# Low parts of 24 weight units moved from GpSimd to VectorE, between GpSimd's indirect DMAs, and TensorE's key units written as loops

## The chip, the core and the metric

The kernel runs on one core of a Trainium2 chip. The metric is the device time of one execution in microseconds (us). Engines are named as in the profile: PE is TensorE, DVE VectorE, ACT ScalarE, POOL GpSimd, SP SyncE (it only issues DMAs here). "L509" is line 509 of the kernel before.

## The reference, cut to what matters

Two transformer blocks over 512 tokens of width 1024, in float32. The change lies in the second half of the first block, a product-key expert layer:

```
q = (ht @ wq).reshape(T, 8, 2, 128)                 # T = 512 tokens
sc = einsum('thpd,hpnd->thpn', q, subkeys)          # 128 scores for each half key
v1, i1 = top_k(sc[:, :, 0], 16);  v2, i2 = top_k(sc[:, :, 1], 16)
best, pos = top_k(v1[..., :, None] + v2[..., None, :], 16)     # 16 experts of each head
experts = e1 * 128 + e2                             # of 16384
gates = softmax(best)
u = u_tab[experts];  vv = v_tab[experts]
act = gelu(einsum('tkd,td->tk', u, x));  out = einsum('tk,tkd->td', gates * act, vv)
```

The kernel does not gather rows of `u_tab`. It computes `gelu(x . u)` of all 16384 experts for all tokens (the **key pass**), and then adds up all rows of `v_tab` weighted by gate times activation (the **value pass**), where the gates stand in a dense, mostly zero table in DRAM. Only for the first 128 tokens does it fetch rows instead. So the gates of the other 384 tokens have to be scattered into that table before the value pass.

## The kernel before, in words

**Units.** Every weight matrix is cut into units of 128 x 1024 float32 (512 KB). Unit `u` goes through a ring of eight buffers: SP loads `raw` (L440) once PE has used unit `u-8`, ACT makes the high part `hi` (L1062, `split_hi`), and POOL or DVE makes the low part `lo = raw - hi`. PE multiplies in three passes, high by high, high by low and low by high (`mm3`, L593 to L595). One unit of the key pass (`project`) is 24 matmuls with 512 columns. ACT writes the gelu of its result to `stage` (L1264, `gelu(u)`), and then makes the high part of unit `u+5`. PE may start unit `u` when the low part of `u` is there and the gelu of `u-4` is done.

**The key pass** is 128 units, `U_PEER` to `U_PEER + 127`; below they are key units 0 to 127. Low parts of key units 0 to 27 (`LOW_FROM` = 28) are POOL's, in four quarters of 256 columns (L509). From 28 on they are DVE's (L1765, `unit_low`), in one instruction, except for the 24 units of the list `BESIDE` (30, 34, 38, 42, 47, 51, ... 123, 127), which are POOL's.

**DVE** has an order written out by hand. It selects the experts of each group of 128 tokens, in the order 1, 2, 3, 0: `select(t, between)` finds the 16 best, and `join_gates(t, between)` sums the gates of equal experts and makes the scatter's addresses; its last step is `gates_made` (after L1863). `between` says how many key units' low parts are made at each step (`lows(n)`). ACT does an exp in between for each `t`, after the gelus of units 5, 17, 29 and 45. After the last select, DVE takes one low part and two parts of the second block's modulation (`ada_part`, L1781 and L1783, on weights that SP loads beside the units) for each unit from 56 on. PE sums these up in between (`ada_sum`, L786), twelve times.

**POOL** issues 384 indirect DMAs (`scatter`, L547), one for each `t` in 1 to 3 and each of 128 slots, each with 128 values of 4 bytes. They come in 24 groups of 16 (`SCATTERS`): a group waits for `gates_made` of its `t`, or for the landing of the group before it of the same `t`. The first five groups are of t = 1, 2, 1, 2, 3. Behind every fourth DMA of a group stands a quarter of the low part of that group's `BESIDE` unit; at the first quarter POOL waits for the high part of that unit.

**The end of the key pass.** After the gelu of unit 124 (`LOADS_AT`) ACT waits for all 384 scatters, then issues the first loads of gates and activations (L1274, L1280), and only then does the gelus of units 125 to 127. DVE multiplies gates by activations (L1921) and makes their low part (L1927), after which PE can start the value pass. PE's value pass is a loop of eight units (`pe.Fori(0, P // RING - 2)`, 14 rounds) between eight units written out at each end. The key pass is written out in full. Then POOL picks activations (L533) and fetches rows (L541) for the first 128 tokens, and the second block follows.

Of the kernel before, what the change touches and what calls it, by code (L numbers as in the profile page):

```python
# [16 lines left out]
F32 = mybir.dt.float32  # L17
# [4 lines left out]
ALU = mybir.AluOpType  # L22
AX_X = mybir.AxisListType.X

P = 128
D = 1024
DC = D // P
# [30 lines left out]
U_DIFF = U_PEER + 2 * P  # L58
# [19 lines left out]
EXP_AT = (5, 17, 29, 45)  # L78
SCATTERS = [(1, 0), (2, 0), (1, 1), (2, 1)] + [s for h in range(6) for s in ((3, h), (1, h + 2), (2, h + 2))] \
    + [(3, 6), (3, 7)]  # L80
BESIDE = [30 + 17 * n // 4 for n in range(len(SCATTERS))]
ZEROS = 8
LOADS_AT = P - 4
BUNCH = 4
# [34 lines left out]
def build_program(nc, w_units, x_in, ctx_in, params, consts, consts2, trig, pool_w, subkeys, ada_w, out,  # L119
                  rel_dram, gate_dram, act_dram, x_dram):  # L120
    KB = 1024
    with ExitStack() as ctx:
# [381 lines left out]

        @block.gpsimd
        def _(pool):
            def quarter(u, part):
                cols = slice(part * (D // 4), (part + 1) * (D // 4))
                return nc.gpsimd.tensor_tensor(lo[:, u % RING, cols], raw[:, u % RING, cols],  # L509
                                               hi[:, u % RING, cols].bitcast(F32), ALU.subtract)  # L510

            def low_part(u, per=0, i=None):

                pool.wait_ge(hi_ready, u + 1 if i is None else i * per + (u + 1))
                for part in range(4):
                    last = quarter(u, part)
                last.then_inc(lo_ready, 1)

            def low_range(a, b):
# [31 lines left out]
            nc.gpsimd.memset(zero[:, :], 0.0).then_inc(zero_made, 1)  # L551
            low_range(0, U_PEER + LOW_FROM)
            pool.wait_ge(zeroed, 16 * ZEROS)
            for n, (t, h) in enumerate(SCATTERS):
                if h == 0:
                    pool.wait_ge(gates_made, t)
                else:
                    pool.wait_ge(scattered[t - 1], 16 * TOPK * h)
                for k in range(TOPK):
                    scatter(t, TOPK * h + k)  # L560
                    if k % 4 == 3:
                        if k == 3:
                            pool.wait_ge(hi_ready, U_PEER + BESIDE[n] + 1)
                        last = quarter(U_PEER + BESIDE[n], k // 4)
                last.then_inc(lo_ready, 1)
            pool.wait_ge(mine_at, 2)
            pool.wait_ge(unit_used, U_VALUES)
            for s in a_stored:
# [15 lines left out]
        def _(pe):  # L584
# [11 lines left out]

            def unit_in(u, per=0, i=None):
                made, n = lo_ready, u + 1
                before = sum(U_PEER + b < u for b in BESIDE)
                if u - U_PEER in BESIDE:  # L600
                    n = U_PEER + LOW_FROM + before + 1
                elif U_PEER + LOW_FROM <= u < U_DIFF + LAG:
                    made, n = value_lo_ready, u + 1 - (U_PEER + LOW_FROM) - before
                elif u >= U_DIFF + LAG:
                    n -= U_DIFF + LAG - (U_PEER + LOW_FROM) - before
                pe.wait_ge(made, n if i is None else i * per + n)

            def project(u, dst, ah, al, per=0, i=None, ready=None):

                unit_in(u, per, i)  # L610
                for c in range(DC):
                    if ready is not None:
                        pe.wait_ge(ready[0], ready[1] + c + 1)
                    wh, wl = unit_chunk(u, c)
                    last = mm3(dst, wh, wl, ah[:, c], al[:, c], c == 0, c == DC - 1)
                last.then_inc(unit_used, 1)
# [157 lines left out]
            scores(2 * PEER_HEADS - 1)  # L774


            def ada_sum(s):

                pe.wait_ge(ada_used, DC * (s + 1))
                if s >= 2:  # L780
                    pe.wait_ge(ada_turned, s - 1)
                sides = range(2 if s < 2 else 1)
                for v in sides:
                    rows = acc[:, s % 2, v].rearrange("p (b q r) -> p q b r", q=4, r=32)
                    for q in range(4):
                        last = mm(ps[32 * q:32 * q + 32, 6 + s % 2, 0:2 * P].rearrange("p (b r) -> p b r", r=32),  # L786
                                  pick_c[:, v, :], rows[:, q], start=v == 0, stop=v == sides[-1])
                last.then_inc(ada_summed, 1)

            pe.wait_ge(cact_ready, 1)  # L790
            for u in range(P):
                if u >= 4:
                    pe.wait_ge(gel_done, u - 3)
                project(U_PEER + u, ps[:, u % 4, :], hn_hi, hn_lo)
                if u == CTX_SQUARE + DC + 2:
                    pe.wait_ge(sq_added, (DC - 1) * (WHOLE[3] + 1))
                    mm(ps[:, 4, 0:TC], ones, csq[:, 0, :], start=True, stop=True).then_inc(mean_ready, 1)
                s, after = (u - ADA_LOW - 3) // 4, (u - ADA_LOW - 3) % 4
                if s == 0 and after == 0:
                    pe.wait_ge(tk_done, 2 * PEER_HEADS)  # L800
                if after == 0 and 0 <= s < SECTIONS:
                    ada_sum(s)

            def value_unit(v, i=None, first=False, final=False):

# [708 lines left out]
        def _(dve):  # L1514
# [285 lines left out]
            def lows(n):  # L1800

                for u in range(key_lows[0], min(key_lows[0] + n, P + LAG)):
                    if u not in BESIDE:
                        unit_low(U_PEER + u)
                key_lows[0] += n

            def select(t, between):
# [80 lines left out]
            select(1, 0)  # L1888
            join_gates(1, (0,) * 7)
            select(2, 0)  # L1890
            join_gates(2, (0, 0, 0, 0, 0, 0, 1))
            select(3, 2)
            join_gates(3, (1, 1, 2, 1, 1, 2, 1))
            select(0, 2)
# [450 lines left out]
```

## Time and profile before

| | |
|---|---|
| median of 3 runs | 3061.32 us (3044.7 to 3061.61) |
| the profiled execution | 3072.2 us, its span 3070.4 us |
| PE busy | 2875.8 us (94%) |
| DVE busy | 1762.4 us (57%) |
| POOL busy | 1704.7 us (56%) |
| ACT busy | 983.9 us (32%) |
| mean granted clock of PE | 0.968 |

The span is from the first to the last instruction; times in views count from its start. A row of the view by lines names line, engine, operation, tiles written and read, their count, then busy time and mean duration, then the idle time before them and what ended it. Spans of POOL are rough, but the start of one indirect DMA to the start of the next is not.

### The profile page before, as it was taken

How to read it: one execution, taken by the hardware profiler on the slowest of the kernel's cores; microseconds unless marked ns; L12 is line 12 of the kernel's file. 1: busy time of each engine (PE TensorE's matmuls, PEld its weight loads, DVE VectorE, ACT ScalarE, POOL GpSimd, SP SyncE). 2: the span in 40 equal slices, each digit the busy share in tenths (PEclk: the TensorE clock that was granted, in tenths of full speed). 3: DMA queues.
4: the chain of work that ended last, by engine and by line, in shares of the span. 5: the costliest groups of instructions: out<-in, count | busy, mean ns of one | idle time of the engine just before them, and what ended most of it. 6: DMA issues, size and time to landing. Idle time of an engine off the chain costs nothing.

```text
span 3070.4 us, 39204 instructions
## 1 busy us (share of the span) xinstructions
PE 2875.8 (94%) x14484; PEld 2443.1 (80%) x14484; DVE 1762.4 (57%) x2726; ACT 983.9 (32%) x1472; POOL 1704.7 (56%) x1757
## 2 busy tenths in 40 slices
PE   8799988888989988999999989999999989999999
PEld 6698877677777778999999858558888868898887
DVE  6568997665553136778887773674333353343333
ACT  4432322222222333333333433783322222232211
POOL 5144877788888755688753123002554545555553
PEclk9899999999999999999999999999999999999999
DMA  6932443378875467999997211101323323233332
GB/s 202 342 97 83 153 129 98 122 250 284 289 267 186 124 209 283 325 338 347 355 350 276 90 55 50 38 1 59 97 90 102 96 76 96 72 108 103 97 95 75
DMA packets 191662, 499.40 MB, mean 163 GB/s; under 512 B 29608, under 2 KB 80936, under 8 KB 190888
## 3 DMA queue, kind: packets, MB, share of 16 engines
q1 hardware_dynamic: 104528, 338.95, 33.4%
q10 hardware_dynamic: 52184, 91.23, 8.4%
q0 software_dynamic: 34816, 67.41, 6.3%
q8 instruction: 86, 1.41, 0.2%
q14 instruction: 48, 0.39, 0.0%
HBM read 432.82 MB, written 64.68 MB: 162 GB/s over the span
## 4 chain that ended last, share of the span: by engine, by line
PE 57%; POOL 21%; DVE 11%; issue 6%; ACT 3%; DMA 2%; another core or an unknown queue 0%; SPq 0%; ACTq 0%; DVEq 0%
PE ps L593 17%; PE ps L595 17%; PE ps L594 17%; POOL gate_dram L547 13%; POOL value_rows L541 3%; POOL picked L533 3%; POOL unit_lo L509 3%; PE ps L917 2%; DVE nb L2000 1%; PE ps L937 1%; DMA unit_raw<-w_units 1%; DVE same L1858 1%; DVE same L1856 1%; DVE gate_sums L1860 1%; PE ps L928 1%
## 5 line engine op out<-in xcount | busy, mean ns | idle before, releaser
L509 POOL TENSOR_TENSOR unit_lo<-unit_raw,unit_hi 128x256 fp32r<-128x256 f32 x1112 | 876.5, 820 | 1049.3 <-ACT unit_hi L1062 1046.5
L593 PE MATMUL ps<-hn_hi,unit_hi 128*128 128x512 f32 (+1 forms) x2344 | 922.8, 394 | 107.3 <-POOL unit_lo L509 74.1
L594 PE MATMUL ps<-hn_lo,unit_hi 128*128 128x512 f32 (+1 forms) x2344 | 904.6, 386 | 0.0
L595 PE MATMUL ps<-hn_hi,unit_lo 128*128 128x512 f32 (+1 forms) x2344 | 903.9, 386 | 0.0
L1062 ACT ACTIVATE unit_hi<-unit_raw 128x1024 fp32r<-128x1024 f32 x486 | 505.7, 1055 | 487.2 <-DMA unit_raw<-w_units 372.8
L593 PEld LDWEIGHTS ps<-hn_hi,unit_hi 128*128 128x128 f32 x2344 | 449.2, 192 | 218.6 <-issue 103.0
L594 PEld LDWEIGHTS ps<-hn_lo,unit_hi 128*128 128x128 f32 x2344 | 449.5, 192 | 88.9 <-issue 4.9
L547 POOL DMA_INDIRECT gate_dram<-gate_sums,gate_at x384 | 460.6, 1199 | 104.1 <-issue 103.4
L595 PEld LDWEIGHTS ps<-hn_hi,unit_lo 128*128 128x128 f32 x2344 | 448.3, 191 | 87.8
L1765 DVE TENSOR_TENSOR unit_lo<-unit_raw,unit_hi 128x1024 fp32r<-128x1024 f32 x208 | 259.8, 1250 | 185.9 <-ACT unit_hi L1062 150.1
L593 PE MATMUL ps<-gp_hi,unit_hi 128*128 128x384 f32 x1024 | 349.2, 341 | 18.2 <-DVE gp_lo L1927 14.2
L595 PE MATMUL ps<-gp_hi,unit_lo 128*128 128x384 f32 x1024 | 346.8, 339 | 3.9 <-issue 3.9
L594 PE MATMUL ps<-gp_lo,unit_hi 128*128 128x384 f32 x1024 | 346.9, 339 | 3.1 <-issue 3.0
L1264 ACT ACTIVATE stage<-ps 128x512 f32<-128x512 f32 x128 | 76.5, 598 | 610.1 <-PE ps L595 570.8
L541 POOL DMA_INDIRECT value_rows<-w_units,row_at x128 | 191.1, 1493 | 123.5 <-DVE own_values L1945 79.8
L2128 DVE TENSOR_TENSOR pf<-gel,ps 128x512 f32<-128x512 f32 x44 | 30.3, 688 | 380.8 <-PE ps L595 380.8
L593 PEld LDWEIGHTS ps<-gp_hi,unit_hi 128*128 128x128 f32 x1024 | 195.6, 191 | 24.0 <-DVE gp_lo L1927 13.8
L533 POOL DMA_INDIRECT picked<-act_dram,act_at x128 | 176.0, 1375 | 62.4 <-issue 38.7
L595 PEld LDWEIGHTS ps<-gp_hi,unit_lo 128*128 128x128 f32 x1024 | 195.6, 191 | 4.8 <-issue 4.8
L594 PEld LDWEIGHTS ps<-gp_lo,unit_hi 128*128 128x128 f32 x1024 | 195.8, 191 | 4.6 <-issue 4.6
L1945 DVE SCALAR_TENSOR_TENSOR own_values<-value_rows,picked,own_values 128x1024 f32<-128x1024 f32 x127 | 162.8, 1282 | 51.3 <-DMA value_rows<-w_units,row_at 40.3
L1481 ACT ACTIVATE gel<-ps 128x512 f32<-128x512 f32 x44 | 26.4, 599 | 495.4 <-PE ps L595 495.4
(280 smaller groups left out, 3862.4 us busy)
## 6 DMA issues: line engine op xcount, KB each, us to landing
unit_raw<-w_units SPq DMA_DIRECT2D x486, 512.0 KB
araw<-ada_units SPq DMA_DIRECT2D x96, 512.0 KB
act_dram<-stage ACTq DMA_DIRECT2D x32, 1024.0 KB
gate_dram<-zero SPq DMA_DIRECT2D x8, 3072.0 KB, 23.6
gbuf<-gate_dram ACTq DMA_DIRECT2D x16, 1536.0 KB
abuf<-act_dram ACTq DMA_DIRECT2D x32, 768.0 KB
gate_dram<-gate_sums,gate_at POOLq DMA_INDIRECT x384
x<-x_t SPq DMA_DIRECT2D x8, 256.0 KB, 6.1
```

The costliest lines, as they stand in the source:

```text
L509: return nc.gpsimd.tensor_tensor(lo[:, u % RING, cols], raw[:, u % RING, cols], hi[:, u % RING, cols].bitcast(F32), ALU.subtract)
L533: pool.indirect_dma_start(picked[:, k:k + 1], None, act_dram.rearrange("u j (t o) -> (u j t) o", o=1), bass.IndirectOffsetOnAxis(act_at[:, ...
L541: pool.indirect_dma_start(vrows[:, k % ROWS, :], None, w_units.rearrange("u p n -> (u p) n"), bass.IndirectOffsetOnAxis(row_at[:, k:k + 1] ...
L547: pool.indirect_dma_start(gate_dram.rearrange("i j (t o) -> (i j t) o", o=1), bass.IndirectOffsetOnAxis(gidx[:, t - 1, k:k + 1], 0), gsum[ ...
L593: mm(dst, wh, ah, start=start, stop=False)
L594: mm(dst, wh, al, start=False, stop=False)
L595: return mm(dst, wl, ah, start=False, stop=stop)
L917: last = mm(SD[m][:, keys], Qd[rows, 4 * m + h // 2, qt * P:(qt + 1) * P], Kd[rows, 4 * m + h // 2, keys], start=True, stop=True)
L1062: activation(hi[:, u % RING], raw[:, u % RING], ACT.Copy).then_inc(hi_ready, 1)
L1264: activation(stage[:, g % 2, u % BUNCH], ps[:, u % 4, :], ACT.Gelu).then_inc(gel_done, 1)
L1765: V.tensor_tensor(lo[:, u % RING], raw[:, u % RING], hi[:, u % RING].bitcast(F32), ALU.subtract).then_inc(value_lo_ready, 1)
L1945: last = V.scalar_tensor_tensor(own[:, :], vrows[:, k % ROWS, :], picked[:, k:k + 1], own[:, :], ALU.mult, ALU.add)
```

## The change

Three edits. **POOL**: the quarters between the scatters go; the 16 DMAs of a group follow each other, and the groups too. `BESIDE` is gone. **DVE**: `lows` makes the low part of every key unit from 28 on, so the 24 units come back in their place in its order. In the join of t = 2 there are now low parts at the last two steps, one and two, where there was one at the last; the other counts stay, and now count the units that were skipped. **PE**: the key units 28 to 51 and 68 to 99 are loops of eight units, of three and four rounds; the others are still written out. Waits for counts are computed from the loop's index. The wait for the units' low parts is simpler, as all of 28 to 127 count on DVE's semaphore.

```diff
@@ POOL
             low_range(0, U_PEER + LOW_FROM)
             pool.wait_ge(zeroed, 16 * ZEROS)
-            for n, (t, h) in enumerate(SCATTERS):
+            for t, h in SCATTERS:
                 if h == 0:
                     pool.wait_ge(gates_made, t)
                 else:
                     pool.wait_ge(scattered[t - 1], 16 * TOPK * h)
                 for k in range(TOPK):
                     scatter(t, TOPK * h + k)
-                    if k % 4 == 3:
-                        if k == 3:
-                            pool.wait_ge(hi_ready, U_PEER + BESIDE[n] + 1)
-                        last = quarter(U_PEER + BESIDE[n], k // 4)
-                last.then_inc(lo_ready, 1)
@@ PE
-            for u in range(P):
+            def key_unit(u, i=None):
+
                 if u >= 4:
-                    pe.wait_ge(gel_done, u - 3)
-                project(U_PEER + u, ps[:, u % 4, :], hn_hi, hn_lo)
-                if u == CTX_SQUARE + DC + 2:
+                    pe.wait_ge(gel_done, u - 3 if i is None else i * RING + (u - 3))
+                project(U_PEER + u, ps[:, u % 4, :], hn_hi, hn_lo, RING, i)
+                if i is None and u == CTX_SQUARE + DC + 2:
...
+            for u in range(LOW_FROM):
+                key_unit(u)
+            with pe.Fori(0, 3) as i:
+                for k in range(RING):
+                    key_unit(LOW_FROM + k, i)
+            for u in range(LOW_FROM + 3 * RING, LOW_FROM + 5 * RING):
+                if u == ADA_LOW + 3:
                     pe.wait_ge(tk_done, 2 * PEER_HEADS)
-                if after == 0 and 0 <= s < SECTIONS:
-                    ada_sum(s)
+                key_unit(u)
+            with pe.Fori(0, 4) as i:
+                for k in range(RING):
+                    key_unit(LOW_FROM + 5 * RING + k, i)
+            for u in range(LOW_FROM + 9 * RING, P):
+                key_unit(u)
@@ DVE
                 for u in range(key_lows[0], min(key_lows[0] + n, P + LAG)):
-                    if u not in BESIDE:
-                        unit_low(U_PEER + u)
+                    unit_low(U_PEER + u)
                 key_lows[0] += n
...
-            join_gates(2, (0, 0, 0, 0, 0, 0, 1))
+            join_gates(2, (0, 0, 0, 0, 0, 1, 2))
```

## Rows read from the trace of the kernel before

**Rows 1.** The page's chain of work that ended last, by engine.
```profile
PE 57%; POOL 21%; DVE 11%; issue 6%; ACT 3%; DMA 2%; another core or an unknown queue 0%; SPq 0%; ACTq 0%; DVEq 0%
```

**Rows 2.** Waits from 421 to 1107 us: waiter, releaser, total, times, longest.
```profile
PE ps L593 <- POOL unit_lo L509: 70.9, 20, 8.4
PE ps L593 <- DVE unit_lo L1765: 10.5, 2, 5.7
```

**Rows 3.** ACT's instructions in order of time: start, us (idle before in brackets).
```profile
540.45 0.60 ACT L1264 ACTIVATE stage<-ps 128x512 f32<-128x512 f32 x1 [3.89 <-PE ps L595]
545.88 0.60 ACT L1264 ACTIVATE stage<-ps 128x512 f32<-128x512 f32 x1 [3.89 <-PE ps L595]
...
560.76 0.60 ACT L1264 ACTIVATE stage<-ps 128x512 f32<-128x512 f32 x1 [13.33 <-PE ps L595]
```

**Rows 4.** Engines by stretch: length, busy of each (count), PE clock, DMA share, GB/s.
```profile
340.00:380.00 40.00, 40.00 (x179) 33.10 (x178) 39.16 (x29) 11.06 (x15) 36.01 (x31) 1.00 0.42 129
421.00:1107.00 686.00, 601.72 (x2583) 482.06 (x2581) 379.58 (x429) 168.16 (x220) 551.60 (x481) 0.94 0.60 195
620.00:660.00 40.00, 38.77 (x171) 31.64 (x169) 32.85 (x27) 10.82 (x14) 33.86 (x28) 1.00 0.89 321
```

**Rows 5.** POOL's work by lines from 421 to 1107 us.
```profile
L547 POOL DMA_INDIRECT gate_dram<-gate_sums,gate_at x384 | 460.6, 1199 | 104.1 <-issue 103.4 <-DMA gate_dram<-gate_sums,gate_at 0.7
L509 POOL TENSOR_TENSOR unit_lo<-unit_raw,unit_hi 128x256 fp32r<-128x256 f32 x97 | 92.7, 955 | 30.4 <-ACT unit_hi L1062 28.3
```

**Rows 6.** Order of time: the first scatter, the last ones, and what follows.
```profile
421.44 1.14 POOL L547 DMA_INDIRECT gate_dram<-gate_sums,gate_at  x1 [0.18 <-issue]
...
1077.83 1.23 DVE L1765 TENSOR_TENSOR unit_lo<-unit_raw,unit_hi 128x1024 fp32r<-128x1024 f32 x1 [4.21 <-issue]
1077.93 1.95 POOL L547 DMA_INDIRECT gate_dram<-gate_sums,gate_at  x1 [0.30 <-issue]
...
1105.45 0.95 POOL L547 DMA_INDIRECT gate_dram<-gate_sums,gate_at  x1 [0.30 <-issue]
...
1108.38 0.39 ACTq L1274 DMA_DIRECT2D gbuf<-gate_dram  x1
...
1119.79 0.51 PE L593 MATMUL ps<-gp_hi,unit_hi 128*128 128x384 f32 x1 [4.07 <-DVE gp_lo L1927]
```

**Rows 7.** ACT at 442 us, the gelu of key unit 27.
```profile
442.05 0.60 ACT L1264 ACTIVATE stage<-ps 128x512 f32<-128x512 f32 x1 [3.89 <-PE ps L595]
```

**Rows 8.** PE's sums of the modulation by lines, 500 to 1010 us.
```profile
L786 PE MATMUL ps<-ada_sums,pick_c 128*32 128x256 f32 x112 | 8.5, 389 | 0.0
```

**Rows 9.** DVE in order of time about the end of the second join.
```profile
445.47 1.23 DVE L1765 TENSOR_TENSOR unit_lo<-unit_raw,unit_hi 128x1024 fp32r<-128x1024 f32 x1
446.61 0.28 DVE L1862 TENSOR_SCALAR sel<-expert,con 128x128 f32<-128x128 f32 x1
446.92 0.23 DVE L1863 TENSOR_SCALAR gate_at<-sel 128x128 int32<-128x128 f32 x1
...
458.81 1.22 DVE L1765 TENSOR_TENSOR unit_lo<-unit_raw,unit_hi 128x1024 fp32r<-128x1024 f32 x1
```

**Rows 10.** Stretch from there to the third join's end, columns as in rows 4.
```profile
447.30:546.90 99.60, 83.66 (x336) 67.27 (x335) 81.81 (x117) 23.98 (x31) 79.39 (x65) 0.90 0.35 104
```

**Rows 11.** The scatters alone by stretch: length, POOL busy (count), clock, DMA share, GB/s.
```profile
421.00:500.00 79.00, 47.02 (x35) 0.86 0.38 113
500.00:1107.00 607.00, 413.52 (x350) 0.95 0.62 206
```

**Rows 12.** The scatters' durations in ns: min/median/max, first and last start.
```profile
L547 POOL DMA_INDIRECT gate_dram<-gate_sums,gate_at x384: 954/983/2850, 421.4 to 1105.5; - x192
```

**Rows 13.** Sixteen picks in a row, from 1130 to 1152 us: durations as in rows 12.
```profile
L533 POOL DMA_INDIRECT picked<-act_dram,act_at x16: 940/948/1897, 1130.8 to 1151.5; - x16
```

**Rows 14.** DVE's waits from 421 to 1107 us.
```profile
DVE unit_lo L1765 <- ACT unit_hi L1062: 130.6, 22, 18.9
DVE ada_sums L1783 <- DMA araw<-ada_units: 71.7, 48, 8.4
```

**Rows 15.** PE's waits from 1130 to 1690 us, the value pass.
```profile
PE ps L593 <- DVE gp_lo L1927: 10.1, 8, 2.2
PE ps L595 <- issue: 3.9, 5, 2.0
PE ps L593 <- issue: 3.9, 7, 1.6
PE ps L594 <- issue: 3.0, 4, 1.6
```

More of the change, by code:

```diff
@@ L80 @@
     + [(3, 6), (3, 7)]
-BESIDE = [30 + 17 * n // 4 for n in range(len(SCATTERS))]
 ZEROS = 8
@@ L506, in _ @@
         def _(pool):
[L507 to L510, printed above, removed]
             def low_part(u, per=0, i=None):
@@ L515, in low_part @@
                 for part in range(4):
-                    last = quarter(u, part)
+                    cols = slice(part * (D // 4), (part + 1) * (D // 4))
+                    last = nc.gpsimd.tensor_tensor(lo[:, u % RING, cols], raw[:, u % RING, cols],
+                                                   hi[:, u % RING, cols].bitcast(F32), ALU.subtract)
                 last.then_inc(lo_ready, 1)
@@ L598, in unit_in @@
                 made, n = lo_ready, u + 1
[L599 to L603, printed above, removed]
+                if U_PEER + LOW_FROM <= u < U_DIFF + LAG:
+                    made, n = value_lo_ready, u + 1 - (U_PEER + LOW_FROM)
                 elif u >= U_DIFF + LAG:
-                    n -= U_DIFF + LAG - (U_PEER + LOW_FROM) - before
+                    n -= U_DIFF + LAG - (U_PEER + LOW_FROM)
                 pe.wait_ge(made, n if i is None else i * per + n)
@@ L774, in _, with ada_sum @@
             scores(2 * PEER_HEADS - 1)
-            def ada_sum(s):
-                pe.wait_ge(ada_used, DC * (s + 1))
+            def ada_sum(s, i=None):
+                pe.wait_ge(ada_used, DC * (s + 1) if i is None else i * (2 * DC) + DC * (s + 1))
                 if s >= 2:
-                    pe.wait_ge(ada_turned, s - 1)
+                    pe.wait_ge(ada_turned, s - 1 if i is None else i * 2 + (s - 1))
                 sides = range(2 if s < 2 else 1)
@@ L788, in ada_sum @@
                 last.then_inc(ada_summed, 1)
-            pe.wait_ge(cact_ready, 1)
-            for u in range(P):
+            def key_unit(u, i=None):
                 if u >= 4:
-                    pe.wait_ge(gel_done, u - 3)
-                project(U_PEER + u, ps[:, u % 4, :], hn_hi, hn_lo)
-                if u == CTX_SQUARE + DC + 2:
+                    pe.wait_ge(gel_done, u - 3 if i is None else i * RING + (u - 3))
+                project(U_PEER + u, ps[:, u % 4, :], hn_hi, hn_lo, RING, i)
+                if i is None and u == CTX_SQUARE + DC + 2:
                     pe.wait_ge(sq_added, (DC - 1) * (WHOLE[3] + 1))
@@ L798, in _ @@
                 s, after = (u - ADA_LOW - 3) // 4, (u - ADA_LOW - 3) % 4
-                if s == 0 and after == 0:
-                    pe.wait_ge(tk_done, 2 * PEER_HEADS)
-                if after == 0 and 0 <= s < SECTIONS:
-                    ada_sum(s)
+                if after == 0 and 0 <= s < SECTIONS:
+                    ada_sum(s, i)
+            pe.wait_ge(cact_ready, 1)
+            for u in range(LOW_FROM):
[5 more added lines that the diff above has]
+                if u == ADA_LOW + 3:
+                    pe.wait_ge(tk_done, 2 * PEER_HEADS)
+                key_unit(u)
[4 more added lines that the diff above has]
+                key_unit(u)
             def value_unit(v, i=None, first=False, final=False):
```

## The prediction

> **What bounds the kernel now.** First the chain of work that ended last [rows 1]: POOL holds a fifth of it, though it does no large computation. Then who waited for whom between the first scatter and the end of the key pass [rows 2]: PE waited 70.9 us in 20 waits for low parts from POOL, and 10.5 us in two waits for DVE. Then ACT's gelus, which mark the ends of PE's units [rows 3]: 5.43 to 5.44 us from one to the next, and 14.88 us where the second is a unit of `BESIDE` (42). Last the stretches [rows 4]: from 340 to 380 us PE is never idle, at a granted clock of 1.00 (2.4 GHz); from 421 to 1107 it is busy 602 of 686 us, at 0.94. A stall so costs twice, by its idle time and by a slow clock (1.2 GHz) after it.
>
> The reason stands in POOL's rows [rows 5]. For a group it issues 16 DMAs of 1.20 us with about 0.30 between, and four quarters of 0.96: 27.8 us. PE wants 4.25 units meanwhile (BESIDE's spacing), 23.1 us. PE therefore follows POOL. The pass ends on POOL as well [rows 6]: the last scatter starts at 1105.45 and ends at 1106.40, ACT issues the first gate load at 1108.38, and PE's first value matmul is at 1119.79, 13.4 us after the last scatter's end.
>
> So the value pass starts 13.4 us after POOL's last scatter or when PE is through with its key units, whichever is later. I work out both.
>
> **PE's side.** The gelu of unit 27 is at 442.05 [rows 7], and 100 units remain. At 5.44 us they take 544 us, the modulation sums 8.5 us [rows 8] (a little more for those outside that window: I take 9). Left-over stalls: unit 28's low part came at 445.47, when PE had waited since 442 [rows 9]. It now stands one join step earlier, about 438.5 (the step takes three DVE operations of 2.3 us), in time. Units 29 and 30 follow at about 446, where 29 had come at 458.81. But units 31 and 32 come in the middle of the next select, as long after its start as 29 did before, and the start is 2.3 us later: about 461, against PE's need at 458.9. I allow 7 us for this stall with its clock. Sum: 442 + 544 + 9 + 7 = 1002 us for the end of unit 127.
>
> The 24 low parts on DVE cost 24 x 1.23 = 30 us there. What hides them: DVE waited 130.6 us in these 686 us for high parts to exist [rows 14], so it is ahead. From 447.3 to 546.9, in the third select and join, it was busy 81.8 of 99.6 us [rows 10] for 13 low parts; now there are 17, so 81.8 + 4 x 1.15 = 86.4 us for 17 units that PE needs 92.5 us for. That is near even; if DVE's operations stretch by a tenth, PE stalls here. The SP queue is not passed by anything that moves. A faster PE asks for more data: at full pace in the modulation stretch the DMA share was 0.89 at 321 GB/s [rows 4], so it holds at that pace, and the earlier stall-free pieces are the evidence.
>
> **POOL's side.** The first scatter stays at 421.44; its group of 16 ends near 445. The gates of t = 2 were made at 447.15 and now have two more low parts ahead: 449.5, so POOL waits some 4 us. Three groups at the early rate, 47.02/35 + 0.30 = 1.64 us [rows 11], take 79 us to about 529. The gates of t = 3 come at 449.5 + 86.4 + 1 = 537, so POOL waits again. **From 537** there are 320 scatters. At the later rate, 413.5/350 = 1.18 + 0.30 = 1.48 us, they take 474 us: 1011.
>
> Two corrections. A scatter runs 0.96 us alone, as most do [rows 12], and 1.95 when it begins with a DVE low part [rows 6]: operations on DVE with two inputs hold it up. Of the moved low parts some 17 lie after 537; a scatter that is already under way when the low part starts loses less than the full 0.99, and a few fall between scatters, so I take 0.6 us for each: 10 us. The DVE work that was there already now meets a scatter more often, as POOL is in one 1.25 of 1.55 us (81%) instead of 461 of 686 us (67%): the excess of 320 x (1.18 - 0.96) = 70 us grows by a fifth, 14 us; I take 10, since low parts and scatters met often already. One more microsecond for the last two groups, both of t = 3, of which the second waits for the landing of the first. Sum: 1011 + 10 + 10 + 1 = **1032 us**, mean 1.55 us for each.
>
> POOL is the later one, by 30 us. ACT waits after the gelu of 124 (about 985) until 1034, and PE idles once from 1002 to 1032 + 13.4 = **1046 us**, where the value pass began at 1119.8: 74 us earlier. The PE stalls of 81 us and their clock are removed, but half of what they were comes back as one wait for the scatters. The slow clock after that wait replaces the slow clock now seen at the same place.
>
> **What the SBUF page says.** The Trainium skill, SBUF — State Buffer, section Who interferes with whom, says that a VectorE `tensor_tensor` takes only the shared pair's read interface, and infers that descriptor generation, which needs the write interface, is not held up by it. By that rule the scatters would all run at the 0.96 us of a quiet one. The row with 1.95 us beside a DVE tensor_tensor disagrees, so the sum goes by the rows.
>
> **TensorE's loops.** Bound from both sides: the value pass is a loop of 14 rounds, and all its waits for issue are 10.8 us in 16 [rows 15]. For the new loops (5 jumps back, 2 entries) that is between nothing and 10.8 for each of the seven, 76 us. I take nothing on the end, because 30 us of PE's slack cover up to three such entries and the 14 rounds together show only one price. A gain by loops I exclude: PE's only waits in the key pass are those for low parts [rows 2].
>
> **The rivals.**
> - *PE is last* (0.08). DVE delays scatters less than I think. Sixteen picks in a row ran at a median of 0.95 [rows 13], from 1130.8 to 1151.5; at 1.26 us the 320 scatters end at 940, and PE's 1002 plus its 4.1 us wait for the first product sets the start: 1006, 114 us earlier, 2947.
> - *The loops stall* (0.06). At 10.8 us for each of seven, PE ends at 1078, starts the value pass at 1082: 38 us earlier, 3023. Against it: [rows 15]. The Trainium skill, Runtime: NRT & Kernel Launch, section Instruction fetch mechanics, speaks for it: a taken branch whose target is outside the fetch window must fetch it first, so unrolling is preferred.
> - *DVE and POOL hold each other up more* (0.15). At the early rate of 1.64 for all 320 and gates of t = 3 at 545: 1070, 36 us earlier, 3025. For it: the early stretch has the dense DVE work that all of the pass gets now.
> - *No change* (0.08): a mean spacing of 1.68 to 1.88 us, since 537 + 320 x 1.78 = 1106 is where the last scatter ends now.
> - *Slower* (0.06). Every scatter lands behind a DVE operation at 1.95 + 0.30 = 2.25: 537 + 720 = 1257, 151 us later, 3212. It decides from a spacing of 1.88 us up. Place: the modulation stretch, where DVE has least idle time. Against it: the median scatter was undisturbed [rows 12].
>
> **The numbers.** The forecast has 0.57. The profiled execution took 3072.2 us, 10.9 above the median, so its own time would be 2998; on the median, 3061.3 - 74 = **2987**. The range takes in the first rival's end and the third's: 2947 to 3025, which leaves out about 2 in 10. A change of 1% (31 us) is what a measurement tells from none. Faster by over 1%: 0.57 + 0.08 + 0.06 + 0.15 = 0.86. Same: 0.08. Slower: 0.06.
>
> **What would show it.** Right: no waits of PE for POOL's low parts; gelus every 5.44 us from 35 to 124 (6.2 behind a modulation sum); scatters with a mean spacing near 1.55; ACT waiting some 45 us after the gelu of 124; one idle stretch of PE of about 45 us before the value pass, which starts near 1046. Wrong: many PE waits for DVE's low parts between units 31 and 60, waits for issue at the loops, or no idle stretch before the value pass.

## The result and the profile after

The changed kernel took 2961.15 us, the median of 4 runs (2943.11 to 2970.1); the kernel before, beside it, 3056.2 (4 runs). The ratio is 0.9686, 95% interval [0.9631, 0.9742]. The forecast was 2987 in a range of 2947 to 3025. In a later session the same kernel took 2954.69 (6 runs), 0.9661 [0.9622, 0.97]. On another chip this did not hold: a median of 3182.39 (6 runs, 3067.7 to 3342.98) beside 3058.77 for the kernel before, 4% more. A ratio with an interval rests only on the executions within 1.5% of a kernel's quickest: here on two of the six, 1.0074 [1.0001, 1.0146]. The first two sessions are the case that was forecast; the third has a part of its own below, with a new wait that scatters the times of one kernel on one chip by up to 9%.

The profiled execution took 2970.1 us with a span of 2968.3, 102.1 less than before. By PE's first value matmul, at 1022.0 instead of 1119.8, it is 97.8 us ahead; the value pass takes 7.3 us less (566.1 instead of 573.4), and what surrounds both 3.0 more.

The chain of waits by engine (against [rows 1]):
```profile
PE 56%; POOL 22%; DVE 11%; issue 7%; ACT 2%; DMA 1%; ACTq 0%; SPq 0%; DVEq 0%
```
The shares are almost unchanged: POOL is still a fifth. It now stands there for its scatters alone.

PE's waits from 421 to 1022 us (against [rows 2]): waiter, releaser, total, times, longest.
```profile
PE ps L584 <- DVE unit_lo L1767: 3.3, 1, 3.3
```
Where there were 22 waits of 81.4 us, there is one of 3.3. No wait is put down to issue, though the loops jump back five times. By stretch (columns as in [rows 4]):
```profile
425.00:1006.00 581.00, 577.64 (x2601) 470.16 (x2600) 386.91 (x453) 168.13 (x220) 455.80 (x385) 0.99 0.69 230
540.00:1006.00 466.00, 466.00 (x2123) 378.60 (x2123) 274.89 (x316) 134.89 (x178) 365.43 (x320) 1.00 0.74 253
```
PE is busy 577.6 of 581 us at a clock of 0.99; before it was 601.7 of 686 at 0.94. The second row has exactly the last 320 scatters: 365.43/320 = 1.142 us each. The gelus stand 5.44 us apart, 6.24 behind a modulation sum:
```profile
712.56 0.60 ACT L1266 ACTIVATE stage<-ps 128x512 f32<-128x512 f32 x1 [3.89 <-PE ps L586]
718.00 0.60 ACT L1266 ACTIVATE stage<-ps 128x512 f32<-128x512 f32 x1 [3.89 <-PE ps L586]
724.24 0.60 ACT L1266 ACTIVATE stage<-ps 128x512 f32<-128x512 f32 x1 [4.70 <-PE ps L586]
```
The scatters as one group (ns: min/median/max, first and last start, then what their engine waited for):
```profile
L543 POOL DMA_INDIRECT gate_dram<-gate_sums,gate_at x384: 954/962/3034, 425.5 to 1004.2; - x192
its engine sat idle before it (us, times) until:
  issue: 116.3, 382
  DVEq L1865: 5.9, 1
```
The end of the key pass in order of time (against [rows 6]):
```profile
1004.22 0.95 POOL L543 DMA_INDIRECT gate_dram<-gate_sums,gate_at  x1 [0.30 <-issue]
...
1006.56 0.39 ACTq L1276 DMA_DIRECT2D gbuf<-gate_dram  x1
...
1008.17 7.78 ACTq L1282 DMA_DIRECT2D abuf<-act_dram  x1
1016.00 0.60 ACT L1266 ACTIVATE stage<-ps 128x512 f32<-128x512 f32 x1 [23.02 <-issue]
...
1022.00 0.66 PE L584 MATMUL ps<-gp_hi,unit_hi 128*128 128x384 f32 x1 [14.29 <-DVE gp_lo L1928]
```
The last scatter ends at 1005.2 and PE's last key matmul at 1007.7. PE then idles once, 14.3 us, until gates can be used: the value pass starts 16.8 us behind the last scatter. So POOL's side still decides, but by little.

### The profile page after: what moved, and what is told of

Same layout as the page of the kernel before. It is cut to its first block, busy times and chain, and to the rows that moved or that the text cites. A ratio compares the mean times of both kernels' runs of the same rounds, so it can differ in the third digit from the quotient of the medians.

```text
span 2968.3 us, 39214 instructions
## 1 busy us (share of the span) xinstructions
PE 2843.7 (96%) x14484; PEld 2425.6 (82%) x14484; DVE 1769.8 (60%) x2750; ACT 986.7 (33%) x1472; POOL 1630.3 (55%) x1661
## 4 chain that ended last, share of the span: by engine, by line
PE 56%; POOL 22%; DVE 11%; issue 7%; ACT 2%; DMA 1%; ACTq 0%; SPq 0%; DVEq 0%
PE ps L584 16%; PE ps L586 16%; PE ps L585 16%; POOL gate_dram L543 12%; POOL picked L529 6%; POOL value_rows L537 5%; PE ps L919 2%; DVE nb L2001 1%; PE ps L939 1%; DVE same L1859 1%; DVE same L1857 1%; DVE gate_sums L1861 1%; PE ps L930 1%; DMA unit_raw<-w_units 1%; DMA value_rows<-w_units,row_at 1%
## 5 line engine op out<-in xcount | busy, mean ns | idle before, releaser
L511 POOL TENSOR_TENSOR unit_lo<-unit_raw,unit_hi 128x256 fp32r<-128x256 f32 x1016 | 785.4, 810 | 1026.1 <-ACT unit_hi L1064 1025.4
L584 PE MATMUL ps<-hn_hi,unit_hi 128*128 128x512 f32 (+1 forms) x2344 | 910.8, 389 | 26.1 <-DVE hn_lo L1634 10.9
L585 PE MATMUL ps<-hn_lo,unit_hi 128*128 128x512 f32 (+1 forms) x2344 | 895.2, 382 | 0.0
L586 PE MATMUL ps<-hn_hi,unit_lo 128*128 128x512 f32 (+1 forms) x2344 | 894.9, 382 | 0.0
L1064 ACT ACTIVATE unit_hi<-unit_raw 128x1024 fp32r<-128x1024 f32 x486 | 506.0, 1055 | 446.1 <-DMA unit_raw<-w_units 339.6
L584 PEld LDWEIGHTS ps<-hn_hi,unit_hi 128*128 128x128 f32 x2344 | 443.0, 189 | 127.8 <-issue 15.8
L585 PEld LDWEIGHTS ps<-hn_lo,unit_hi 128*128 128x128 f32 x2344 | 443.2, 189 | 87.5 <-issue 4.9
L1767 DVE TENSOR_TENSOR unit_lo<-unit_raw,unit_hi 128x1024 fp32r<-128x1024 f32 x232 | 282.4, 1220 | 127.7 <-ACT unit_hi L1064 126.9
L537 POOL DMA_INDIRECT value_rows<-w_units,row_at x128 | 198.7, 1552 | 98.5 <-DVE own_values L1946 55.8
L529 POOL DMA_INDIRECT picked<-act_dram,act_at x128 | 190.0, 1485 | 62.6 <-issue 38.7
```

The lines of the kernel that those rows point to most:

```text
L511: last = nc.gpsimd.tensor_tensor(lo[:, u % RING, cols], raw[:, u % RING, cols], hi[:, u % RING, cols].bitcast(F32), ALU.subtract)
L529: pool.indirect_dma_start(picked[:, k:k + 1], None, act_dram.rearrange("u j (t o) -> (u j t) o", o=1), bass.IndirectOffsetOnAxis(act_at[:, ...
L537: pool.indirect_dma_start(vrows[:, k % ROWS, :], None, w_units.rearrange("u p n -> (u p) n"), bass.IndirectOffsetOnAxis(row_at[:, k:k + 1] ...
L584: mm(dst, wh, ah, start=start, stop=False)
L585: mm(dst, wh, al, start=False, stop=False)
L586: return mm(dst, wl, ah, start=False, stop=stop)
```

## The experiments

All ratios are against the kernel before on the same chip. The experiments down to the low parts with one input ran on the chip on which the changed kernel took its 2954.69.

**The loops alone.** All 128 key units written out.
```
-            with pe.Fori(0, 3) as i:
-                for k in range(RING):
-                    key_unit(LOW_FROM + k, i)
...
+            for u in range(P):
+                key_unit(u)
```


> The changed kernel with all 128 key units of TensorE written out, no loops. My theory: the loops give nothing and cost nothing on the path; the key units still go at 5.44 us, the value pass starts about 17 us after the last scatter, near 1022 us of the trace, and the time is that of the changed kernel, 2961 us, within 0.5%; ratio to the kernel before 0.964 to 0.974. Rival: 384 indirect DMAs with nothing between them starve TensorE's instruction stream when it is written out; then TensorE waits for issue in the key pass by more than the 14 us of slack it has before the value pass, say 30 us or more, and the ratio is 0.975 or higher. A third outcome: the 10.8 us of waits for issue in the value pass, which the kernel before had and the changed one has not, come back; then 2972 us, 0.972.

2963.6 us, 0.9736 [0.9707, 0.9765]. The units take 5.44 us as in the loops, PE's key units end at 1002.7, the last scatter at 1009.0, the first value matmul is at 1021.9. None of PE's waits is for issue, so the starved instruction stream of the rival did not come on this chip; the written-out kernel was not run on the chips where it came later. The loops cost PE nothing. The ratio is 0.5 to 0.8% above the two of the changed kernel (0.9686, 0.9661), so a small gain by them isn't excluded, but nothing of it shows in PE's units: what is later here is the last scatter. Nearly all that the change brings comes from POOL's quarters.

**The same load on POOL, but nobody waits for it.** An addition of 128x256 on constants after every fourth scatter.
```
+                    if k % 4 == 3:
...
+                        nc.gpsimd.tensor_tensor(spare[:, :], con[:, 0:256], con[:, 128:384], ALU.subtract)\
+                            .then_inc(spare_done, 1)
```


> The changed kernel, but GpSimd again does a tensor_tensor of 128 x 256 after every fourth scatter, on constants into a buffer that nobody reads: no wait for a unit, and nobody waits for it. Theory (the end of the scatters sets the start of the value pass, whoever waits meanwhile): 96 of these at 0.8 to 1.0 us with 0.3 us about them add 80 to 100 us to GpSimd's row; the last scatter ends near 1090 to 1105 us, TensorE is through with its key units near 1008 as in the changed kernel and then idles for about 85 to 100 us, and the time is about 2961 + 90 = 3050, ratio 0.99 to 1.00: the gain is gone although no TensorE wait for a GpSimd low part is back. Rival (the gain came from TensorE no longer waiting for GpSimd's low parts): the time stays near 2961, ratio 0.97.

3046.5 us, 0.9991 [0.9968, 1.0014]. POOL's lines from 421 to 1110 us, then PE at the start of the value pass:
```profile
L545 POOL DMA_INDIRECT gate_dram<-gate_sums,gate_at x384 | 479.6, 1249 | 103.9 <-issue 102.6 <-DMA gate_dram<-gate_sums,gate_at 0.7
L563 POOL TENSOR_TENSOR spare<-con 128x256 f32<-128x256 f32 x96 | 90.3, 941 | 2.1
```
```profile
1111.64 0.66 PE L593 MATMUL ps<-gp_hi,unit_hi 128*128 128x384 f32 x1 [105.85 <-DVE gp_lo L1937]
```
PE is through with its key units at 1005.8 and then stands 105.85 us. The 81 us of waits that the change removed were not the path: only their place was. The kernel gains because 96 operations of 0.94 us (and what they delay) no longer stand between scatters.

**DVE's join counts put back.**
```
-            join_gates(2, (0, 0, 0, 0, 0, 1, 2))
+            join_gates(2, (0, 0, 0, 0, 0, 0, 1))
```


> The changed kernel with the low parts in the second join as before, one at the last step and none at the one before. Theory: TensorE waits about 5 us each for units 28 and 29 again and ends its key units 10 to 15 us later, near 1020; the gates of t = 2 come 2.3 us earlier, those of t = 3 about as before; the last scatter stays near 1005 or 2 us earlier. The slack of 14 us takes most of it: 0 to 6 us more in all, ratio 0.967 to 0.973. Rival: TensorE's delay also delays high parts, so VectorE, so the gates of t = 3, and all 10 to 15 us come through: ratio 0.972 or more.

2958.68 us, 0.9703 [0.9656, 0.975]. PE stalls 9.8 us in two waits for low parts instead of 3.3 in one, and ends its key units at 1010.8; its wait before the value pass is 5.4 instead of 14.3. The stall has moved from the slack at the end to the beginning; the time does not tell the two kernels apart.

**No scatters of t = 3.** A third of the gates is left out.
```
             for t, h in SCATTERS:
+                if t == 3:
+                    continue
...
-                    for s in scattered:
+                    for s in scattered[0:2]:
```


> The changed kernel without the 128 scatters of t = 3, whose gates are then missing from the output: 256 scatters instead of 384, which end near 840 us. Theory: TensorE's key units, which end near 1008, now set the start of the value pass; loads of gates start after the gelu of unit 124 at 991, so the value pass starts at 1010 to 1013 instead of 1022, and only 9 to 12 us are gained: 2950 us, ratio 0.965. Rival (TensorE still has a large reserve of its own): it starts much earlier, and the gain goes to 40 us or more, below 2925.

2934.11 us, 0.9628 [0.9599, 0.9656]. The scatters end at 834, PE's key units at 1005.3, the value pass begins at 1008.0 behind a wait of 2.7 us. So 171 us less of scatters bring 14 us on the start (10 against the changed kernel's other profile, 1017.9, from the same chip): PE is the next bound and lies that close.

**The wait for the scatters moved behind ACT's last gelu**, the activations' loads ahead of it. The second kernel also has two more groups of t = 1 and 2 before the first of t = 3, and other join counts.
```
-LOADS_AT = P - 4
+LOADS_AT = P - 1
...
+                if u == P - 6:
...
+                if u == LOADS_AT:
+                    for s in scattered:
+                        act.wait_ge(s, 16 * SLOTS)
+                    for g in range(2):
+                        load_gates(g)
```


> The changed kernel itself, beside the next ones on the same chip, so that they can be compared with it. Ratio to the kernel before 0.966 to 0.974; the value pass starts near 1022 us.

> The changed kernel, with ScalarE's wait for the scatters moved behind the gelu of unit 127, and the two loads of activations, which need no gate, issued after the gelu of unit 122. Theory: in the changed kernel 16.8 us lie between the last scatter's end and the value pass, of which 9.4 us are the issue of the four loads on ScalarE's queue (7.8 us of it the last one) and 4 us the gelus of 125 to 127 behind it. Both leave the path; what stays is the landing of the first gate load, some 6 us, and the product, high and low part. The value pass starts 8 to 10 us after the last scatter, near 1014: 7 to 9 us are gained, ratio to the changed kernel 0.997. Rival: the four loads share the DMA engines anyway and the first gate load lands no sooner; no difference.

> As the kernel with early loads of activations, and two more edits: two groups of scatters of t = 1 and 2 come before the first of t = 3, so that GpSimd does not wait 6 us for the gates of t = 3, and VectorE makes one more low part at the end of the second join (and one less at the end of the third), so that TensorE does not wait 3.3 us for unit 31. Theory: the last scatter ends 4 to 6 us earlier (a second landing wait of 2 us at the tail takes some back) and TensorE's key units 5 to 6 us earlier, near 1002; the value pass starts near 1008 to 1010, 12 to 14 us before that of the changed kernel: ratio to it 0.995 to 0.996. Rival: TensorE is the bound by then, or VectorE's order shifts the gates of t = 3 later, and nothing comes on top of the early loads.

On one chip: the changed kernel 2954.69 (0.9661 [0.9622, 0.97]), the loads ahead 2945.04 (0.9654 [0.9611, 0.9698]), all of it 2947.52 (0.9641 [0.9603, 0.968]). None of the three can be told from another. With the loads ahead the last scatter ends at 1004.4 and the first value matmul is at 1021.5, 17.1 us later, as in the changed kernel (16.8). DVE's row shows why:
```profile
1019.61 1.03 DVE L1924 TENSOR_TENSOR gp<-abuf,gbuf 128x384 f32<-128x384 f32 x2 [17.28 <-DMA gbuf<-gate_dram]
```
The two gate loads need a median of 15.4 us from issue to landing. From the first one's issue to the first value matmul it is 11.4 us in [rows 6], 15.4 in the changed kernel and 15.4 here, where ACT's last gelus are done before. The theory has fallen, its rival was right. In the kernel with all of it the scatters end at 1000.0 and PE's key units at 996.7; the gate load is issued 5.3 us behind the last scatter, the two land in a median of 6.9 us, and the value pass starts at 1014.2, 3.7 us before the changed kernel's on the same chip (1017.9). It was to be 12 to 14, and the times don't show it. Why the gate loads landed faster there was not tested.

**DVE's low parts with one input.** The low parts are not computed.
```
-                V.tensor_tensor(lo[:, u % RING], raw[:, u % RING], hi[:, u % RING].bitcast(F32),
-                                ALU.subtract).then_inc(value_lo_ready, 1)
+                V.tensor_scalar(lo[:, u % RING], raw[:, u % RING], 0.0, None, ALU.mult).then_inc(value_lo_ready, 1)
```


> The changed kernel, but VectorE makes the low parts of key and value units with a tensor_scalar of the raw unit times zero, so with one input from SBUF instead of two; the low part of these weights is left out of the result. Theory (VectorE's operations with two inputs hold up the scatters): the mean scatter falls from 1.19 to 1.04 to 1.10 us, the last scatter ends 30 to 45 us earlier, near 965, and TensorE, which ends at 1003 to 1008, sets the start: 10 to 14 us gained, 2948. Rival by the Trainium skill, SBUF - State Buffer: tensor_tensor does not hold up descriptor generation and a float32 tensor_scalar, which can run in a mode with both ports, does; then the scatters are as slow or slower, mean 1.19 or more, and the last scatter ends at 1005 or later.

2916.43 us, 0.9534 [0.9485, 0.9583]. The value pass starts 13.2 us earlier, as forecast (1004.7 instead of 1017.9 in the changed kernel beside it). For the scatters the direction is right and the size is not: the last one ends at 988.0 (1001.8), and the 384 have a mean of 1.132 us instead of 1.180, which is neither the theory's 1.04 to 1.10 nor the rival's 1.19 or more. The reason is that the one-input operation holds scatters as well. POOL, then DVE, in order of time:
```profile
975.78 1.41 POOL L543 DMA_INDIRECT gate_dram<-gate_sums,gate_at  x1 [0.31 <-issue]
977.50 0.96 POOL L543 DMA_INDIRECT gate_dram<-gate_sums,gate_at  x1 [0.30 <-issue]
```
```profile
975.67 0.69 DVE L1767 TENSOR_SCALAR unit_lo<-unit_raw 128x1024 fp32r<-128x1024 f32 x1 [3.15 <-ACT unit_hi L1064]
```
It holds them for a shorter time because it is shorter (0.70 instead of 1.22 us), not because it has one input; the figures are in the last section. More of this kernel's gain lies in the value pass, 535.9 us instead of 560.5. There PE waits nine times behind its first matmul for `gp_lo` in the changed kernel, 16.4 us in all, and not once here.

**Low parts in halves**, two operations of 512 columns, alone and with the order of the kernel above; beside them the changed kernel once more.
```
+                for cols in (slice(0, D // 2), slice(D // 2, D)) if u < U_PEER + P else (slice(0, D),):
+                    last = V.tensor_tensor(lo[:, u % RING, cols], raw[:, u % RING, cols],
+                                           hi[:, u % RING, cols].bitcast(F32), ALU.subtract)
```


> The changed kernel, with each low part of the key units on VectorE as two instructions of 512 columns instead of one of 1024; same work, some 0.15 us more for each unit. Theory (a scatter is held only if it starts while a VectorE operation of this kind runs, and then for what is left of it): halves are about 0.69 us, so a scatter is held for less; the delay by a unit's low part falls from about 0.4 to 0.25 us, the mean scatter from 1.18 to about 1.14, the last scatter ends 10 to 18 us earlier against the first one, and no scatter is over 1.7 us where only a low part stands beside it (1.95 before). The value pass starts at 1010 to 1014, bounded by TensorE; about 8 us gained, ratio 0.964 or so. Rival (delay by total overlap, as my forecast had it: 0.6 us for each microsecond together): the mean scatter stays at 1.18 or rises to 1.20, and the last scatter ends no earlier than 1002.

> Halves, together with the early loads of activations, the order of scatters and the low parts' counts of the kernel with all three. Theory: TensorE ends its key units near 998 and the last scatter near 985 to 990; what is left is the landing of the first gate load; the value pass starts near 1002 to 1006, some 16 us before the changed kernel: 2940, ratio to the kernel before 0.961. Rival: the gate load lands 12 us after its issue as before, with the units' loads beside it; value pass at 1008 or later, no gain over 5 us.

> The changed kernel again, beside the two others: ratio 0.966 to 0.970, value pass at 1018 to 1022.

This chip gave a median of 3341.43 us with halves (two of six executions: 1.0669 [1.06, 1.0737]), 3251.89 with halves and order (five of six: 1.0621 [1.0573, 1.0668]), and for the changed kernel itself the 3182.39 of the beginning. The kernel before took 3058.77 there. Nothing can be read of halves; what can be read is a new wait, in all three. The changed kernel's PE waits from 540 to 1000 us:
```profile
PE ps L585 <- issue: 116.0, 53, 2.9
PE ps L586 <- issue: 114.7, 54, 3.6
PE ps L584 <- issue: 106.2, 54, 2.2
```
Before it, in the midst of it and behind it (columns as in [rows 4]):
```profile
500.00:540.00 40.00, 40.00 (x178) 33.15 (x177) 38.20 (x28) 10.98 (x15) 26.75 (x19) 1.00 0.43 130
600.00:900.00 300.00, 62.94 (x108) 31.08 (x108) 13.08 (x13) 6.16 (x8) 229.04 (x232) 0.50 0.05 11
1000.00:1300.00 300.00, 300.00 (x1390) 241.23 (x1389) 190.28 (x185) 82.15 (x107) 0.00 (x0) 1.00 0.82 301
```
In 300 us PE does 108 matmuls instead of 1390. No wait for data is among its waits; DVE, ACT and the loads follow PE and stand with it. POOL and PE in order of time:
```profile
699.87 0.96 POOL L543 DMA_INDIRECT gate_dram<-gate_sums,gate_at  x1 [0.31 <-issue]
700.53 0.29 PEld L584 LDWEIGHTS ps<-hn_hi,unit_hi 128*128 128x128 f32 x1 [1.81 <-issue]
701.13 0.96 POOL L543 DMA_INDIRECT gate_dram<-gate_sums,gate_at  x1 [0.30 <-issue]
701.93 0.58 PE L584 MATMUL ps<-hn_hi,unit_hi 128*128 128x512 f32 x1 [2.20 <-issue]
702.40 0.96 POOL L543 DMA_INDIRECT gate_dram<-gate_sums,gate_at  x1 [0.31 <-issue]
703.33 0.29 PEld L585 LDWEIGHTS ps<-hn_lo,unit_hi 128*128 128x128 f32 x1 [2.51 <-issue]
703.66 0.96 POOL L543 DMA_INDIRECT gate_dram<-gate_sums,gate_at  x1 [0.30 <-issue]
704.73 0.58 PE L585 MATMUL ps<-hn_lo,unit_hi 128*128 128x512 f32 x1 [2.21 <-issue]
```
PE gets one instruction every 1.4 us, a unit of 24 matmuls takes 67.2 us, and the scatters follow one another undisturbed every 1.26. The slow clock (0.50) is not the cause: at that clock weight load and matmul take 0.29 and 0.58 of the 2.8 us. It begins in unit 46 (first issue wait at 557 us) and goes on through the rounds of the first loop (to unit 51) into the written-out units. It outlasts the scatters by 27 us: the last one ends at 960.5, and PE waits for issue until 987.5, with POOL idle. The units 46 to 52 take 434 us instead of 38; the key units end at 1401, where they had at 1007.7. In the kernel with halves it is the same stretch. With halves and order it came from about 690 us on, in units 66 to 72, in the second loop for the most part; shorter spells of 8, 5 and 1 us stand at 473 to 619. So it is tied neither to a jump nor to loops as such; the last experiment has it in written-out units. The two queues that the profile marks as carrying instructions moved one packet (8 KB) from 600 to 900 us: a load of code that PE waited for doesn't show there.

Density alone does not bring it. The changed kernel's scatters in the profile of the result, then here (length, POOL busy, PE clock, DMA share, GB/s):
```profile
850.00:890.00 40.00, 30.56 (x32) 1.00 0.57 176
640.00:680.00 40.00, 30.55 (x32) 0.50 0.15 40
```
In the first PE has no wait for issue.

**A short pause after every fourth scatter.** As the second experiment, with 128x64 instead of 128x256; nothing is left out.
```
-                        nc.gpsimd.tensor_tensor(spare[:, :], con[:, 0:256], con[:, 128:384], ALU.subtract)\
+                        nc.gpsimd.tensor_tensor(spare[:, 0:64], con[:, 0:64], con[:, 128:192], ALU.subtract)\
```


> The changed kernel with a short GpSimd addition of 128x64 on constants, into a buffer that nothing reads, after every fourth scatter (96 of them); nothing is left out. Theory: in the changed kernel's third profile TensorE got its instructions late (units of 67 us instead of 5.44, the idle time put down to issue) while scatters followed one another every 1.26 us without a pause, and a pause after each fourth, as the kernel before had with its 1.2 us quarters, prevents that. Then the key units take 5.44 us to their end at any time, no issue waits stand before their matmuls, and what is left is the price of the additions: 96 of 0.3 to 0.45 us, 29 to 43 us, less what the scatters would have been held up by VectorE anyway; the last scatter ends at 1025 to 1045 us, the first value matmul stands at 1040 to 1060, and the time is 2975 to 3000 us, ratio 0.975 to 0.985, whatever the chip. Rival: the pauses are too short, or it is not their lack that starves TensorE; then on a chip that does it units of over 20 us and issue waits of hundreds of us stay, and the ratio is over 1.0. Where nothing is starved to begin with, both give only the price of the additions, and the run tells nothing of the rival but that price.

This was another chip again. Its 12 executions took 2997.73 to 3105.4 us, median 3070.0, where the kernel before took 3053.67. The ratio of the four quickest (2997.73 to 3029.99) is 0.9866 [0.9826, 0.9905], near the price of the additions; the other eight lie at 3054.55 to 3105.4, and the profiled one is among these. PE's waits from 890 to 1060 us, and three stretches:
```profile
PE ps L595 <- issue: 35.7, 21, 3.6
PE ps L593 <- issue: 30.1, 18, 2.2
PE ps L594 <- issue: 29.6, 21, 2.2
```
```profile
700.00:860.00 160.00, 160.00 (x739) 128.41 (x738) 105.63 (x100) 44.80 (x58) 132.88 (x125) 1.00 0.93 326
862.00:907.00 45.00, 45.00 (x204) 36.42 (x202) 9.70 (x15) 10.82 (x14) 36.22 (x41) 1.00 0.48 152
920.00:1037.00 117.00, 33.68 (x57) 15.86 (x56) 3.67 (x4) 3.69 (x6) 92.41 (x108) 0.50 0.05 13
```
The theory that a pause of this length prevents it has fallen: 95.4 us of issue waits, on a second chip, mostly at 2.1 or 2.8 us from matmul to matmul and with pauses that POOL's rows show (0.33 us, 24 in 130 us). It sits in units 108 to 111, which are written out, and ends 7 us after the last scatter. That the pauses make it rarer may be, since it came 350 us later than in the changed kernel on the chip before, but that is a comparison of two chips and not shown. The stretch ahead of it (862 to 907) is the first after the modulation: DVE is busy 9.7 of 45 us there, so the scatters ran nearly undisturbed.

## Why the prediction was right, point by point

- **What removes the time: right.** The waits for POOL's low parts are gone (22 waits to 1). But the second experiment shows that they weren't what counted; the end of the scatters was, as the prediction had it with its two sides.
- **PE's side: right.** Forecast 1002, measured 1007.7 in an execution where unit 27's gelu came 4.0 us later (446.1); the stall at units 31 and 32 was to be 7 us and was 3.3 in one wait, at 466.
- **POOL up to the gates of t = 3: right.** t = 2 came 27.6 us after the first scatter (28.1 forecast), t = 3 114.8 after (115.6). POOL waited 5.9 us for those of t = 3 (8 forecast) and not at all for those of t = 2 (4 forecast), as its first 16 scatters ran until 453.5.
- **The 320 scatters: mis-sized, by 30 us.** Forecast 1.55 us from one to the next, measured 464.6/320 = 1.452. The failed terms are the two corrections for DVE. Beyond 0.958 us each, the 320 lost 58.9 us; the forecast had 320 x (1.18 - 0.96) + 10 + 10 = 90. In the kernel before the 320 scatters and 7 more from 540 us on had a mean of 384.83/327 = 1.177, so more low parts went with less loss. Scatters that began in one of the 65 low parts of this stretch lost 30.9 us in all before; with 82 low parts they lost 26.9. That is 0.33 us for each low part instead of 0.48, where the forecast had 0.6 for each that was added. Scatters that began in one of the modulation's 112 operations lost 32.7 us before and 23.2 after, where the forecast had DVE's older work cost 10 more. The order of the starts, below, says how each single loss comes about; that scatters and operations meet at better moments now, with 0.67 us of a low part left in the mean instead of 0.87, was forecast by nothing and is luck.
- **The last scatter to the value pass: 16.8 us instead of 13.4**, the landing of the first gate load. It is 12.9 to 18.1 us in the profiles in which the scatters decide; moving ACT's waits alone changed nothing.
- **The end.** The last scatter ended 26.8 us ahead of its forecast of 1032 (30 by the spacing, less 4 for the late first scatter), the gate load took 3.4 more: 23.4 of the 24 us by which the value pass beat 1046 (the sum is 1045.4 before rounding). PE idled 14.3 us ahead of it instead of 45. The value pass itself added 7.3, which no step had; it varies from 549 to 573 us between the profiles of the kernels that compute all of it.
- **The loops: right at nothing**, by the first experiment. The Trainium skill, Runtime: NRT & Kernel Launch, section Instruction fetch mechanics, has a stall for a taken branch whose target must be fetched; the trace shows no wait for issue at the five jumps back.
- **The rival "PE is last"** (0.08) was nearer than the forecast gave it: the fourth experiment puts its start 10 to 14 us away. Its condition, scatters every 1.26 us over hundreds of us, came true only where PE was starved, and there it was the sign of the loss and not of the gain.
- **The rival that was missing.** That PE could be left without instructions while the scatters run stood in no list, and on two chips it decides. That the result comes from a chip where it stayed away is luck. The rows that bore on it were read as a price of loops. Of the 10.8 us of issue waits in [rows 15], 8.1 stand at 1152 to 1163 us, at the end of the sixteen picks of [rows 13] and of four row fetches right behind them, all some 1.25 us apart from 1139 on:
```profile
1158.66 0.48 PE L595 MATMUL ps<-gp_hi,unit_lo 128*128 128x384 f32 x1 [2.00 <-issue]
1160.75 0.48 PE L593 MATMUL ps<-gp_hi,unit_hi 128*128 128x384 f32 x1 [1.61 <-issue]
```
The changed kernel runs the same value loop without a wait for issue, so the loop was not the price. With that reading, the case "slower" would have had a mechanism with a place, and more than 0.06.

## What to carry to other kernels

Work on the engine that issues a chain of DMAs costs its full time if the chain's end decides, whoever waits for the work: look at the end of the chain, not at the waits. What a neighbour's operation costs such a chain depends on which of the two starts first, so read starts and not busy shares. Before a queue of indirect DMAs is made dense, look for issue waits of other engines in the places where it is already dense, and run the result on more than one chip.

## What the runs showed of the hardware

**A scatter is held if it starts while a low part runs on DVE, and for about what is left of that.** POOL, then DVE, in the changed kernel:
```profile
987.32 0.96 POOL L543 DMA_INDIRECT gate_dram<-gate_sums,gate_at  x1 [0.31 <-issue]
988.59 1.04 POOL L543 DMA_INDIRECT gate_dram<-gate_sums,gate_at  x1 [0.30 <-issue]
...
992.46 0.96 POOL L543 DMA_INDIRECT gate_dram<-gate_sums,gate_at  x1 [0.30 <-issue]
993.73 1.34 POOL L543 DMA_INDIRECT gate_dram<-gate_sums,gate_at  x1 [0.30 <-issue]
```
```profile
987.57 1.23 DVE L1767 TENSOR_TENSOR unit_lo<-unit_raw,unit_hi 128x1024 fp32r<-128x1024 f32 x1 [4.15 <-ACT unit_hi L1064]
993.01 1.23 DVE L1767 TENSOR_TENSOR unit_lo<-unit_raw,unit_hi 128x1024 fp32r<-128x1024 f32 x1 [4.21 <-ACT unit_hi L1064]
```
The scatter of 987.32 is under way when the low part starts and takes its 0.96; the next starts 0.21 us before the low part's end and takes 1.04; that of 993.73 starts with 0.51 left and takes 1.34. Over the changed kernel's last 320: 51 scatters that began in a low part, with 0.67 us of it left in the mean, took 0.53 more; 25 in whose midst a low part began took 0.002 more. In the kernel with one-input low parts 47 that began in one, with 0.43 left, took 0.31 more. Scatters that began in a TENSOR_REDUCE, MAX8 or FIND_INDEX8 (2, 5 and 4 of them) took at most 0.01 more. There are exceptions to the order of the starts: three scatters in whose midst a one-input TENSOR_SCALAR of the modulation began, 0.14 to 0.33 us after them, took 0.06 to 0.25 more.

The Trainium skill, SBUF — State Buffer, section Who interferes with whom, says that whichever starts first gets the shared ports for its whole instruction. The trace agrees but for those three: the order of the starts decides. It names `tensor_scalar` among the operations that can take these ports, and the scatter of 1.41 us above agrees. It also infers that a `tensor_tensor` does not hold up descriptor generation; the 0.53 us of the 51 scatters disagree.

**PE can be left without instructions while indirect DMAs run densely.** Issue waits of 95 to 337 us in all were seen in the four profiles that were taken on two chips (four kernels). From the first scatter to the end of the value pass the others have none, but for the 10.8 us beside the picks in the kernel before. That kernel, which has a quarter of 0.96 us after every fourth scatter, had medians of 3058.77 and 3053.67 us on these two chips, as elsewhere; but one of its 17 executions on the second took 3829.72 us at a granted clock of 0.691, and no trace of it was kept, so it can't be said that it is safe. While it lasts the parts hold each other: PE does little, so DVE gets no work, so nothing delays the scatters. That is what the profiles show. That the scatters are the cause is likely from when it comes, but not shown: 32 of them in 40 us left PE at full pace on another chip, and it outlasted them by up to 27 us. What starts it, why it comes on some chips only, and whether the quarters' length or something else about them keeps it away was not settled.
